# A TensorE kernel of two transformer blocks: projection units issued in three passes over their slices

## What is computed

```
for l in range(DEPTH):                                   # first block
    h = hybrid_mixer(x, ...)                             # proj = x @ w_in[l]; ... ; merged @ w_mix_out[l]
    x = layer_norm(ALPHA * x + h, ln1_g[l], ln1_b[l])
    h = memory_cross_attention(x, mem, ...)              # x @ wq, mem @ wkv, o @ wo
    x = layer_norm(ALPHA * x + h, ln2_g[l], ln2_b[l])
    h = conv_ffn(x, ...)                                 # x @ w_up, conv, gelu(a) * b, @ w_down
    x = layer_norm(ALPHA * x + h, ln3_g[l], ln3_b[l])
for layer in range(DEPTH):                               # second block
    x = sandwich(x, c_act, mixer, ...)                   # h @ w_in ... @ w_out
    x = sandwich(x, c_act, mlp, ...)                     # square(relu(h @ w1)) @ w2
```

## Time and profile before

| | |
|---|---|
| median of 3 runs | 4037.62 us (4034.64 to 4044.15) |
| the profiled execution | 4036.18 us, of which 4034.2 us are the span from its first to its last instruction |
| mean granted TensorE clock over the span | 0.959 |
| PE matmuls busy | 3708.1 us, 92% |
| POOL busy | 1850.3 us, 46% |
| DVE busy | 1538.4 us, 38% |
| ACT busy | 1003.2 us, 25% |
| read from HBM | 340.14 MB, 85 GB/s over the span |

### The profile page before, as it was taken

How to read it: one execution, slowest core, us unless ns; L and a number is a source line. 1 busy time by engine, 2 the same in 40 slices (tenths; PEclk the granted TensorE clock), 3 DMA queues, 4 the chain that set the end, 5 groups by cost and what they waited for, 6 DMA issues and landing times.

```text
span 4034.2 us, 45107 instructions
## 1 busy us (share of the span) xinstructions
PE 3708.1 (92%) x18221; PEld 2806.8 (70%) x18221; DVE 1538.4 (38%) x2312; ACT 1003.2 (25%) x1943; POOL 1850.3 (46%) x1218
## 2 busy tenths in 40 slices
PE   7899887999988999879999799998899989989998
PEld 5677765777756776757777566776688767667886
DVE  3454423424134544234342353423543243235332
ACT  1244223212022442132110354333211023212011
POOL 3344552555533345525555344342466533344664
PEclk9999999999989999999999899999899989998998
DMA  4112221655322113215553222221332322122332
GB/s 124 57 58 59 83 84 48 179 167 157 89 63 58 58 53 88 85 47 156 162 165 86 59 59 71 60 71 35 89 94 84 94 73 63 40 81 70 97 90 68
DMA packets 578694, 345.22 MB, mean 86 GB/s; under 512 B 15935, under 2 KB 561976, under 8 KB 578488
## 3 DMA queue, kind: packets, MB, share of 16 engines
q1 hardware_dynamic: 574541, 337.34, 29.1%
q10 hardware_dynamic: 3947, 4.99, 0.4%
HBM read 340.14 MB, written 2.14 MB: 85 GB/s over the span
## 4 chain that ended last, share of the span: by engine, by line
PE 83%; DVE 7%; ACT 5%; POOL 2%; issue 2%; ACTq 0%; DMA 0%; SPq 0%; POOLq 0%; DVEq 0%
PE gemm L216 22%; PE gemm L218 21%; PE gemm L217 21%; PE outs L297 8%; PE scores L297 5%; PE gemm L253 1%; POOL w_low L203 1%; PE scores L1407 1%; PE gemm L254 1%; PE gemm L255 1%; DVE work L1396 1%; ACT tiles L623 1%; POOL w_high L201 1%; DVE tiles L1500 0%; DVE tiles L1497 0%
## 5 line engine op out<-in xcount | busy, mean ns | idle before, releaser
L201 POOL CAST w_high<-w_raw 128x1024 fp32r<-128x1024 f32 (+3 forms) x585 | 549.2, 939 | 2071.5 <-PE gemm L218 1704.7
L203 POOL TENSOR_TENSOR w_low<-w_raw,w_high 128x1024 fp32r<-128x1024 f32 (+3 forms) x585 | 1226.2, 2096 | 46.8
L216 PE MATMUL gemm<-x_high,w_high 128*128 128x512 f32 x2584 | 1052.9, 407 | 49.0 <-POOL w_low L203 37.9
L217 PE MATMUL gemm<-x_low,w_high 128*128 128x512 f32 x2584 | 1018.3, 394 | 0.0
L218 PE MATMUL gemm<-x_high,w_low 128*128 128x512 f32 x2584 | 1018.0, 394 | 0.0
L216 PEld LDWEIGHTS gemm<-x_high,w_high 128*128 128x128 f32 x2584 | 492.9, 191 | 197.1 <-issue 51.0
L216 PE MATMUL gemm<-split_tiles,w_high 128*128 128x512 f32 (+1 forms) x1456 | 585.9, 402 | 24.5 <-DVE split_tiles L531 9.5
L218 PEld LDWEIGHTS gemm<-x_high,w_low 128*128 128x128 f32 x2584 | 491.3, 190 | 108.2
L217 PE MATMUL gemm<-split_tiles,w_high 128*128 128x512 f32 (+1 forms) x1456 | 564.8, 388 | 0.0
L217 PEld LDWEIGHTS gemm<-x_low,w_high 128*128 128x128 f32 x2584 | 492.7, 191 | 103.4 <-issue 6.3
L218 PE MATMUL gemm<-split_tiles,w_low 128*128 128x512 f32 (+1 forms) x1456 | 564.3, 388 | 0.0
(11 more groups left out here) (344 smaller groups left out, 3576.0 us busy)
## 6 DMA issues: line engine op xcount, KB each, us to landing
w_raw<-in_mod_w SPq DMA_DIRECT2D x96, 512.0 KB, 3.7
w_raw<-in_mlp_w SPq DMA_DIRECT2D x96, 512.0 KB, 4.1
w_raw<-in_w_in SPq DMA_DIRECT2D x88, 512.0 KB, 3.8
w_raw<-in_f_w_up SPq DMA_DIRECT2D x88, 512.0 KB, 4.9
w_raw<-in_e_w_in SPq DMA_DIRECT2D x48, 512.0 KB, 3.9
w_raw<-in_o_w_in SPq DMA_DIRECT2D x30, 512.0 KB, 3.9
w_raw<-in_w_branch SPq DMA_DIRECT2D x48, 256.0 KB, 2.7
w_raw<-in_mlp_w SPq DMA_DIRECT2D x32, 384.0 KB, 3.3
```

Of the source, the lines that this page charges most:

```text
L201: me.pool.tensor_copy(WH[:, h, 0:n], W32[:, s, 0:n]).then_inc(sem["pool_done"], 1)
L203: me.pool.tensor_tensor(WL[:, h, 0:n], W32[:, s, 0:n], WH[:, h, 0:n].bitcast(F32), ALU.subtract).then_inc(sem["w_split"], 1)
L216: me.pe.matmul(o, wh, hi, start=begin and k == 0, stop=False)
L217: me.pe.matmul(o, wh, lo, start=False, stop=False)
```

## The change

In unit, the matmuls of one unit are issued in three passes over its slices: first high weights by high activations for all slices, then high weights by low activations for all slices, then low weights by high activations for all slices. A new semaphore, w_rounded, is raised by POOL's cast; PE waits for it ahead of the first pass, and for w_split only ahead of the third. The waits of the list ready stand in the first pass. POOL waits for its own cast through w_rounded in place of pool_done, in unit and in unit_pair; PE's side of unit_pair is as it was. The wait for the bank now stands ahead of the wait for the weights.

```diff
-        names = ["w_read", "w_split", "unit_done", ...
+        names = ["w_read", "w_split", "w_rounded", "unit_done", ...
...
             split = me.tick("w_split")
+            rounded = me.tick("w_rounded")
...
-                me.pool.tensor_copy(WH[:, h, 0:n], W32[:, s, 0:n]).then_inc(sem["pool_done"], 1)
-                me.pool.wait_ge(sem["pool_done"], me.seen("pool_done"))
+                me.pool.tensor_copy(WH[:, h, 0:n], W32[:, s, 0:n]).then_inc(sem["w_rounded"], 1)
+                me.pool.wait_ge(sem["w_rounded"], rounded)
                 me.pool.tensor_tensor(WL[:, h, 0:n], W32[:, s, 0:n], WH[:, h, 0:n].bitcast(F32),
                                       ALU.subtract).then_inc(sem["w_split"], 1)
             if me.pe:
-                me.pe.wait_ge(sem["w_split"], split)
                 if me.bank_freed[bank] is not None:
                     me.pe.wait_ge(sem[me.bank_freed[bank][0]], me.bank_freed[bank][1])
                 o = G[0:cols, bank, 0:N]
+                me.pe.wait_ge(sem["w_rounded"], rounded)
                 for k in range(K):
-                    hi, lo = src(k)
-                    wh = WH[:, h, k * cols:(k + 1) * cols]
-                    wl = WL[:, h, k * cols:(k + 1) * cols]
                     if ready is not None:
                         me.pe.wait_ge(sem["dve_step"], ready[k])
-                    me.pe.matmul(o, wh, hi, start=begin and k == 0, stop=False)
-                    me.pe.matmul(o, wh, lo, start=False, stop=False)
-                    mm = me.pe.matmul(o, wl, hi, start=False, stop=end and k == K - 1)
+                    me.pe.matmul(o, WH[:, h, k * cols:(k + 1) * cols], src(k)[0], start=begin and k == 0, stop=False)
+                for k in range(K):
+                    me.pe.matmul(o, WH[:, h, k * cols:(k + 1) * cols], src(k)[1], start=False, stop=False)
+                me.pe.wait_ge(sem["w_split"], split)
+                for k in range(K):
+                    mm = me.pe.matmul(o, WL[:, h, k * cols:(k + 1) * cols], src(k)[0], start=False,
+                                      stop=end and k == K - 1)
                 mm.then_inc(sem["unit_done"], 1)
```

More of the change, by code:

```diff
@@ L142, in build @@
         O = ctx.enter_context(nc.psum_tensor("outs", [P, 2, S], F32))
-        names = ["w_read", "w_split", "unit_done", "bank_free", "pe_to_dve", "dve_to_pe", "dve_to_act", "act_to_dve",
+        names = ["w_read", "w_split", "w_rounded", "unit_done", "bank_free", "pe_to_dve", "dve_to_pe", "dve_to_act", "act_to_dve",
                  "act_to_pe", "dve_done", "act_done", "pool_done", "in_landed", "dve_to_sp", "out_stored",
@@ L237, in unit_pair @@
                         me.pool.wait_ge(sem["unit_done"], done - HRING)
-                    me.pool.tensor_copy(WH[:, h, 0:K * P], W32[:, s, 0:K * P]).then_inc(sem["pool_done"], 1)
-                    me.pool.wait_ge(sem["pool_done"], me.seen("pool_done"))
+                    me.pool.tensor_copy(WH[:, h, 0:K * P], W32[:, s, 0:K * P]).then_inc(sem["w_rounded"], 1)
+                    me.pool.wait_ge(sem["w_rounded"], rounded)
                     me.pool.tensor_tensor(WL[:, h, 0:K * P], W32[:, s, 0:K * P], WH[:, h, 0:K * P].bitcast(F32),
```

## The result

The changed kernel takes **4019.4 us** as the median of 6 runs (4015.95 to 4022.56), the kernel before 4040.0 in the same comparison (6 runs, 4034.64 to 4049.26): ratio 0.9947, with an interval of 0.9933 to 0.9961. The profiled execution is 4016.2 us with a span of 4014.3, against 4036.2 and 4034.2: 20.0 us less where 29.3 were forecast.

What follows compares the result with a forecast made beforehand. TensorE was taken as the bound, 92% busy, with POOL's weight steps exposed at stops. 32.0 - 8.8 + 7.8 + 1.7 - 3.4 = 29.3 us less gave a forecast of 4008.3 us, range 3998 to 4024.

Steps and rivals of the forecast that it cites:

- rival 1: The clock gives nothing back and the new w_mix_out stop costs the full 3.0 us each: 4020 us, chance 0.17.
- Starts behind the stops: PE starts units at the cast instead of waiting for w_low at the first matmul: 32.0 us gained together.
- the wide stops: Nine PE stops after a unit_pair or a late load of weights, each 2.42 us shorter: 21.8 us gained.
- The four of 1.06: Four 0.89 us stops at the first eight-slice unit after units of four; 4 x 1.06 = 4.2 us gained.
- Ready lists: Units whose slices are just being made have more matmuls left after the last slice: 8.8 us lost.
- the clock in w_mix_out: The first w_mix_out unit's stop grows to 4.5 us and lowers the clock: 2 x 1.7 = 3.4 us lost.
- The clock behind pairs and loads: Clock falls after long stops go or shrink: 7.8 us gained behind three pairs, 1.7 behind late loads.
- The keys: Six small stops at 256-column units of the cross attention, 3.3 us in all: nothing gained, as POOL was never idle.
- rival 3: Gain taken up elsewhere, as loads or DVE and ACT steps don't come earlier: 4023 or 4037.6 us, chance 0.11 together.
- Added waits, order of matmuls: One more PE wait in each of 585 units, and w_high's uses parted by the new order: both taken as zero cost.
- rival 2: The new matmul succession slows 7752 matmuls by 6.6 ns each, 51 us: 4059 us, chance 0.06.
- its fast side: The other 4368 matmuls also run at 226.7 ns: at most 29 us less, 3979 us, chance 0.03.

Runs made afterwards that it cites:

- experiment 1: Changed kernel, but PE waits for w_split ahead of the first pass, as before, so the order alone: 4051.7 us, ratio 1.0034 to the kernel before.
- Experiment 6: Changed kernel with ready-list units slice by slice as before, plus one early ACT gelu on a spare column to load the table: 3987.4 us, one execution.
- experiment 4: Changed kernel, but the x_wq unit behind the pair waits for w_low at its start, in two places: 4022.4 us, ratio 0.9959 to the kernel before.
- experiments 8 and 12: 8: changed kernel, ready lists and keys slice by slice, early gelu with spare column, earlier pair starts, 3981.7 us; 12: same, column made 96 bytes, 3987.1 us.

## Why the prediction was right, and where it was not

The time lay in the range and on the right side, but 4019 is outside the forecast's own bounds of 4003 to 4014 and nearer to the 4020 of rival 1: the range held by what it allowed for the rivals. By steps, from the unit-by-unit comparison of the two profiled executions:

- *Starts behind the stops, 32.0 us.* Measured 27.5. The mechanism is shown by experiment 1, in which the same order without the early start gains nothing. Too large were the wide stops at 47 and 1157 (1.6 us each in place of 2.42), the conv units at 712 and 1828 (1.16 for 1.98) and those at 2886 and 3657 (2.18). **The step that failed** is "At a wide stop PE can start when the cast has landed": the bank is freed later, by a gelu behind its table load, by the taps of the convolution, by the squaring. Experiment 6 shows it for the first two; for the others it is read from the list of waits. The four of 1.06 came to 1.05, x_wq and 3282 to 2.33.
- *Ready lists, 8.8 lost, and the clock in w_mix_out, 3.4 lost.* Measured 10.0 for the two w_mix_out units with their clock (9.7 forecast), 1.5 for x_wo (1.2), 1.3 for the last projection (1.3): 12.8 for 12.2. The last stop was 3.70 us, not 4.5, since part of it now stands ahead of the seventh matmul (2.00).
- *The clock behind pairs and loads, 9.5 gained.* Measured 8.9: the units are 1.6, 2.8 and 2.9 us shorter at the three pairs and 1.6 at 448; the one at 1560 stayed low.
- *The clock elsewhere* was taken as unchanged, and that failed. The cross attention lost 2.4 us in each layer (experiment 4), other places gave and took; the 2.1 us more gained than lost are what is left over in the sum below and were not measured by themselves. As a whole the time at the lower level did not shrink, which is what rival 1 said, though for another reason: the old falls did go, and new ones came.
- *The keys, nothing.* Measured 0.46 us lost in each layer, by the longer cast. PE's earlier end lets ACT and DVE start earlier, beside POOL's cast; that is a small form of rival 3.
- *Sum:* 27.5 - 12.8 + 8.9 - 4.8 - 0.9 + 2.1 = 20.0 us. The first block's two layers end where they did before; the whole gain is in the second block, which has no w_mix_out and no cross attention.
- *Added waits, order of matmuls.* Three successive matmuls of a unit on x_high and x_low take 683.2 ns before and 683.8 after, 227.7 each where the forecast took 226.7 from two units, so rival 2 is refuted for the order, and a weight load is still needed for each one. But its fast side, "the other 4368 at 226.7", was a real possibility that had nothing to do with the order: an address reaches 229.1.

## What to carry to other kernels

When a wait is moved later, list everything else that the instruction waits for, the PSUM bank first: the next of them ends the stop. Passes over slices belong where all operands are there; where slices come one at a time, the order by slices leaves the least work behind the last one. And before one credits an edit with 0.5%, one looks at the spacing of the matmuls on each operand and at the granted clock place by place: the spacing that came with an unused column of 4 bytes was worth 12.4 us here, more than half of what the change gave, and one program's executions differed by 20 us through the clock.

## What was not expected of the hardware

- The pace of fp32r matmuls with 512 columns depends on where the moving operand lies in SBUF: 229.1 or 233.2 ns for the same program, with an unused column as the only difference. Two more placements gave no rule.
- Shorter stops do not mean more clock. With a stop of 3 us ahead of the cross attention it ran at 1.00 in all four kernels that have one; without the stop it fell to 0.50 in seven and stayed at 1.00 in three. Over kernels of nearly the same work the time at the lower level, without the first 40 us, went from 297 to 350 us. Which stretches fall changes with an edit that moves work by a microsecond, even with the width of an unused column (experiments 8 and 12).
- The Trainium skill ("TensorE: Matmul & The Clock Gate", Part 1: The HAM clock gate) says that the gate goes by how busy TensorE has been lately; by that alone a kernel with less idleness should spend less time at the lower level. The trace differs: 338.3 us for 332.9, and in experiment 4, with an added stop, the attention behind it ran at the full clock. The measurement decides.
- DVE's step with two SBUF operands and POOL's steps slow each other. In the changed kernel the low part that starts at 587.43 takes 1.64 in place of 0.74 us, beside POOL's subtraction, which runs until 588.53, and the cast that starts at 588.46 takes 1.50 in place of 1.04. A low part that starts inside a subtraction takes 2.18 us in the kernel before too, and the subtraction 2.68 in place of 2.39. The Trainium skill ("GPSIMD Engine Reference", 1. Specifications) says that GpSimd's way into SBUF is shared with VectorE, and that instructions of VectorE with two SBUF inputs contend for it; the trace agrees.
